# Issuing the loads of the weight sums from GpSimd's queue in the down projection of a hybrid block

## The reference, cut to what matters

```
n2 = rmsnorm(x, norm_ffn_g[l])
gate, up = jnp.split(n2 @ w_up[l], 2, axis=-1)
gate = causal_dwconv(gate, ffn_conv_w[l], ffn_conv_b[l])
x = x + (jax.nn.silu(gate) * up) @ w_down[l]
return rmsnorm(x, norm_final_g)
```

## Time and profile before

| what | us |
|---|---|
| median of 3 runs | 1129.65 |
| lowest and highest of them | 1127.28, 1418.37 |
| the profiled execution | 1126.34 |
| its span, first to last instruction | 1124.5 |
| PE, DVE, ACT, POOL busy | 1103.8, 878.1, 625.3, 53.3 |
| SP's queue of transfers, share of the 16 DMA engines | 80.1% |
| POOL's queue of transfers, the same | 0.5% |

### The profile page before, as it was taken

How to read it: one execution, slowest core, us unless ns; L and a number is a source line. 1 busy time by engine, 2 the same in 40 slices (tenths; PEclk the granted TensorE clock), 3 DMA queues, 4 the chain that set the end, 5 groups by cost and what they waited for, 6 DMA issues and landing times.

```text
span 1124.5 us, 16379 instructions
## 1 busy us (share of the span) xinstructions
PE 1103.8 (98%) x5938; PEld 946.2 (84%) x5938; DVE 878.1 (78%) x1144; ACT 625.3 (56%) x794; POOL 53.3 (5%) x46
## 2 busy tenths in 40 slices
PE   8999999999999999999999999999999999999995
PEld 8888888888888888888888888888888878777774
DVE  6778586785875677887888778788877888899796
ACT  7656475564756554344444444444444677677784
POOL 0100000000000000000000000000000000000300
PEclk9999999999999999999999999999999999999999
DMA  8877778778475578899899888988997988888984
GB/s 257 253 221 245 236 222 269 225 223 263 160 236 176 178 233 254 278 300 288 265 289 298 283 268 290 296 272 268 304 295 253 319 303 307 283 287 288 327 299 146
DMA packets 186727, 293.94 MB, mean 261 GB/s; under 512 B 9228, under 2 KB 151824, under 8 KB 182976
## 3 DMA queue, kind: packets, MB, share of 16 engines
q1 hardware_dynamic: 185664, 291.15, 80.1%
q0 software_dynamic: 448, 1.78, 0.5%
q10 hardware_dynamic: 576, 0.53, 0.1%
HBM read 261.96 MB, written 31.46 MB: 261 GB/s over the span
## 4 chain that ended last, share of the span: by engine, by line
PE 83%; DVE 9%; DMA 5%; ACT 2%; issue 1%; SPq 1%; DVEq 0%; ACTq 0%
PE ps L1465 42%; PE ps L1467 21%; PE ps L1600 12%; PE ps L1649 3%; DVE s_w L1222 2%; PE ps L1462 2%; DVE w L1222 2%; DVE w L868 2%; DMA s_raw<-w_down_dram 1%; DMA raw<-sums 1%; PE ps L1463 1%; ACT w L543 1%; DMA xres<-x_dram 1%; DMA raw<-w_down_dram 1%; DVE s_act L1222 1%; PE ps L1576 1%
## 5 line engine op out<-in xcount | busy, mean ns | idle before, releaser
L1465 PE MATMUL ps<-xT,w 128*128 128x512 f32 x2048 | 715.5, 395 | 0.6 <-DVE w L868 0.6
L543 ACT ACTIVATE w<-raw 128x1024 fp32r<-128x1024 f32 (+3 forms) x377 | 392.8, 1058 | 331.5 <-PE ps L1467 171.6
L1467 PE MATMUL ps<-xT,w 128*128 128x256 f32 x2048 | 569.1, 278 | 0.0
L868 DVE TENSOR_TENSOR w<-raw,w 128x1024 fp32r<-128x1024 f32 x332 | 407.4, 1243 | 185.9 <-ACT w L543 185.2
L1465 PEld LDWEIGHTS ps<-xT,w 128*128 128x128 f32 x2048 | 384.1, 188 | 90.0 <-issue 0.7
L1467 PEld LDWEIGHTS ps<-xT,w 128*128 128x128 f32 x2048 | 385.0, 188 | 0.3
L1600 PE MATMUL ps<-w,aT 128*128 128x512 f32 x768 | 176.9, 390 | 5.5 <-DVE aT L874 5.5
L1600 PEld LDWEIGHTS ps<-w,aT 128*128 128x128 f32 x768 | 143.2, 188 | 38.0 <-DVE w L868 7.1
L1649 PE MATMUL ps<-s_w,s_act 128*128 128x512 f32 x336 | 80.4, 394 | 2.2 <-DVE s_act L1222 2.1
L1649 PEld LDWEIGHTS ps<-s_w,s_act 128*128 128x128 f32 x336 | 62.6, 188 | 18.3 <-DVE s_act L1222 5.0
L1222 DVE TENSOR_TENSOR s_w<-s_raw,s_w 128x1024 fp32r<-128x1024 f32 (+1 forms) x48 | 65.7, 1395 | 3.6 <-ACT s_w L543 3.5
(11 more groups left out here) (177 smaller groups left out, 632.5 us busy)
## 6 DMA issues: line engine op xcount, KB each, us to landing
raw<-w_up_dram SPq DMA_DIRECT2D x176, 512.0 KB, 5.8
raw<-w_in_dram SPq DMA_DIRECT2D x92, 512.0 KB, 4.3
s_raw<-w_down_dram SPq DMA_DIRECT2D x72, 512.0 KB, 7.9
sums<-s_raw SPq DMA_DIRECT2D x56, 512.0 KB, 6.5
raw<-w_down_dram SPq DMA_DIRECT2D x44, 512.0 KB, 5.6
raw<-w_out_dram SPq DMA_DIRECT2D x32, 512.0 KB, 4.6
s_raw<-sums SPq DMA_DIRECT2D x16, 1024.0 KB, 7.5
raw<-sums SPq DMA_DIRECT2D x12, 1024.0 KB, 7.4
```

Of the source, the lines that this page charges most:

```text
L543: return sc.activation(out_, in_, fn, **kw)
L868: v.tensor_tensor(w[:, s, :, 1, :], raw[:, s, :].rearrange("p (c n) -> p c n", c=CH), w[:, s, :, 0, :], ALU.subtract).then_inc(lo_ready, 1)
L1465: mm(full, w[:, s, c, 0, cut], xT[:, kt, :, :].rearrange("p a n -> p (a n)"), start=kt == 0, stop=False)
L1467: ins = mm(rest, w[:, s, c, 1, cut], xT[:, kt, 0, :], start=False, stop=kt == KT - 1)
```

## The change

The sums of all 28 pairs are now loaded by instructions in POOL's queue (`load_sums`), with the same waits as before on DVE's steps. SP's `load_pair` issues the plain weights alone and no longer waits for the four steps. The wait on `t_stored` moves from SP to POOL. POOL's order in the down projection becomes: wait for the stored sums; sums of both runs of the first half; sums of the first run of the second half; sums of the first pair of the second run; the load of `gfin`; `xg` for r = 0; `xg` for r = 1; sums of the other six pairs. The waits of `gfin` and `xg` keep their values.

```
--- before.py
+++ after.py
@@ -304,6 +304,10 @@
 
             return 1, m, i
 
+        def sums_place(half, run, i):
+
+            return run * (2 * RUN_PAIRS) + (half * RUN_PAIRS + i)
+
         up_pairs = [(half, run, i) for half in range(2) for run in range(RUNS) for i in range(RUN_PAIRS)]
         for i in range(H):
             for m in range(MIX_SUMS if i < H - 1 else 1):
@@ -391,10 +395,6 @@
 
             down_rows = w_down.rearrange("(k p) n -> k p n", p=P)
 
-            def sums_place(half, run, i):
-
-                return run * (2 * RUN_PAIRS) + (half * RUN_PAIRS + i)
-
             def load_for_sums(half, run, i):
 
                 k = run * RUN_TILES + (RING + 2 * i)
@@ -417,7 +417,6 @@
                 dst = pair_raw[place]
                 upper = down_rows[bass.ds(k, 1), :, cols + BANK:cols + HALF].rearrange("k p n -> p (k n)")
                 lower = down_rows[bass.ds(k + 1, 1), :, cols:cols + HALF].rearrange("k p n -> p (k n)")
-                sums = sums_dram[bass.ds(sums_place(half, run, i), 1)].rearrange("t p n -> p (t n)")
                 if i == 1:
                     g = LAST_BODY[run] + (G_DOWN + half * DOWN_BODIES)
                     sp.wait_ge(lo_ready, g * RING + (RING + 2))
@@ -427,13 +426,6 @@
                     sp.wait_ge(s_lo_ready, p * S_PARTS + (1 - S_PARTS))
                 sp.dma_start(dst[:, 0:BANK], upper).then_inc(plain_landed[place], 16)
                 sp.dma_start(dst[:, BANK:BANK + HALF], lower).then_inc(plain_landed[place], 16)
-                if i == 1:
-                    sp.wait_ge(lo_ready, g * RING + 2 * RING)
-                elif i:
-                    sp.wait_ge(s_lo_ready, p * S_PARTS - S_PARTS)
-                elif half or not at_start(run):
-                    sp.wait_ge(s_lo_ready, p * S_PARTS)
-                sp.dma_start(dst[:, 2 * HALF:4 * HALF], sums).then_inc(sums_landed[place], 16)
 
             COL_Q, COL_K, COL_V, COL_O, COL_XR, COL_GR = 0, D_M, 2 * D_M, 3 * D_M, 4 * D_M + 2 * H, 4 * D_M + 2 * H + D_L
             wa_v = wa.rearrange("(i b) k j -> i k b j", b=2)
@@ -511,7 +503,6 @@
             if len(up_pairs) == UP_ITERS - 1:
                 store_sums(2 * PAIRS - 1, *up_pairs[-1])
             load_body(G_DOWN, w_down, 0, 0)
-            sp.wait_ge(t_stored, 32 * 2 * PAIRS)
 
             def load_pairs(half, run):
 
@@ -1403,16 +1394,46 @@
             with pool.Fori(0, UP_ITERS) as j:
                 after(pool, A3, "silu", j)
                 did(nc.gpsimd.tensor_tensor(fs[:], fs[:], rB[:].to_broadcast([P, 2, S]), ALU.mult), L3, "fs_r")
-            pool.wait_ge(s_used, S_STEPS * (PAIRS + RUN_PAIRS))
-            pool.dma_start(gfin, gfin_in.to_broadcast([P, D])).then_inc(gfin_landed, 16)
-            pool.wait_ge(gfin_landed, 16)
-            for r in range(ROWS):
+
+            def load_sums(half, run, i):
+
+                place, p = place_of(i), nth_pair(half, run, i)
+                if i == 1:
+                    g = LAST_BODY[run] + (G_DOWN + half * DOWN_BODIES)
+                    pool.wait_ge(lo_ready, g * RING + 2 * RING)
+                elif i:
+                    pool.wait_ge(s_lo_ready, p * S_PARTS - S_PARTS)
+                elif half or run:
+                    pool.wait_ge(s_lo_ready, p * S_PARTS)
+                pool.dma_start(pair_raw[place][:, 2 * HALF:4 * HALF], sums_dram[sums_place(half, run, i)]).then_inc(sums_landed[place], 16)
+
+            def load_gfin():
+
+                pool.wait_ge(s_used, S_STEPS * (PAIRS + RUN_PAIRS))
+                pool.dma_start(gfin, gfin_in.to_broadcast([P, D])).then_inc(gfin_landed, 16)
+
+            def weigh(r, b):
+
+                pool.wait_ge(gfin_landed, 16)
                 after(pool, A4, f"sq{r}_0")
-                pool.wait_ge(unit_used, (G_DOWN + DOWN_BODIES + r + 1) * RING + (RING + 3))
+                pool.wait_ge(unit_used, (G_DOWN + DOWN_BODIES + b) * RING + (RING + 3))
                 for n in range(2):
                     cols = slice(n * BANK, (n + 1) * BANK)
                     ins = nc.gpsimd.tensor_tensor(xg[:, r, cols], xres[:, r, cols], gfin[:, cols], ALU.mult)
                 did(ins, L4, f"xg{r}")
+
+            pool.wait_ge(t_stored, 32 * 2 * PAIRS)
+            for run in range(RUNS):
+                for i in range(RUN_PAIRS):
+                    load_sums(0, run, i)
+            for i in range(RUN_PAIRS):
+                load_sums(1, 0, i)
+            load_sums(1, 1, 0)
+            load_gfin()
+            weigh(0, 1)
+            weigh(1, 2)
+            for i in range(1, RUN_PAIRS):
+                load_sums(1, 1, i)
 
 
         @block.tensor
```

## The result

| | before | after |
|---|---|---|
| median, us | 1129.4 | 1144.44 |
| lowest, us | 1127.28 | 1141.88 |
| profiled execution and its span, us | 1126.34, 1124.5 | 1144.79, 1142.5 |

The change makes the kernel slower: 1.0135 times the time before, with an interval of 1.0111 to 1.0158. That is 15 us, against 7 us in the sum of the forecast, and just outside its range of 1125 to 1144 us.

A forecast was written before the change was run, and what follows sets the result against it. PE, busy 98% of the span, was taken as the bound, with DVE and DMA nearly full in the pairs. 1126.34 + 6.2 + 1.0 = 1133.5 us profiled, 1135 us expected as median; range 1125 to 1144 us.

The forecast's parts named there:

- Removed from SP: 28 issues of sums leave SP's queue with their waits; costed at nothing, at most some 0.3 us gain for a pair.
- The first sums: Down projection's first sums, issued after POOL's last up-projection product, land before ACT needs them: 0, at worst 0.9 us.
- The sums of a run's first pair: Issued earlier by POOL, they move beside body-weight loads at the second half's start: +1.0 us, bounds 0 to 3.5 us.
- The price of one load from POOL: Two loads of sums in the chain cost the same from POOL as from SP: 0, bounds +4.6 to -5.1 us.
- The sums behind `xg`: Last run's second-pair sums wait in POOL behind both `xg` steps, issued 10.2 us later: +6.2 us, 5.4 to 8.8.
- The clock: PE's granted clock might fall to 1.2 GHz after some 5.1 us idle in the last run: 0, 2.6 us in range.
- POOL's descriptors held by DVE: Rival: DVE delays POOL's descriptor making up to 4 us per load of sums, giving 1165 us; chance 0.09.
- Hiding: Rival: PE's stock hides the late sums of the last run's second pair, giving 1127.3 us; chance 0.06.
- gain: Rival: two queues land loads sooner and shed PE's waits in the pairs, 1126.6 or 1121 us; chance 0.15.

The follow-up runs named there:

- run 1: Not a follow-up kernel: the first of four runs of pairs in the down projection; 35.6 us in the kernel before, 37.3 us in the changed kernel.
- both parts undone: Changed kernel with `xg` for r = 1 moved behind the last six pairs' sums and early first-pair sums held back: 1.0063 times the kernel before, 7.1 us slower.
- 20 loads: Kernel before with the sums of pairs three to seven of each run loaded from POOL, `xg` for r = 1 behind them: ratio 1.0065, 7.3 us slower.
- run 4: Not a follow-up kernel: the last of four runs of pairs in the down projection; 36.2 us in the kernel before, 43.3 us in the changed kernel.
- undoing the order: Changed kernel with `xg` for r = 1 moved in POOL's order behind the loads of the last six pairs' sums: 1.0103 times the kernel before.
- The three early loads: Kernel before with first-pair sums of runs two to four issued early, from POOL (1.0036), ACT (1.0043) or SP behind the body's loads (0.9990).

## Why the prediction was wrong, by its own steps

- *Removed from SP*: nothing was forecast, and no run tests it alone.
- *The first sums*: POOL issued them at 879.38 us, 1.3 us behind the forecast by the later start of the whole; run 1 has no wait that hangs on them.
- *The sums of a run's first pair*: the step that failed first. I asked how long 1 MB takes (3.5 us) and then chose 1.0 us at one place, because the load "starts last". It doesn't: POOL issued it at 984.98 and 1047.41 us, and the body load in the chain began at 985.08 and 1047.52 us. It reached the body's last units in two places, not one, and the stages there are 4.1 and 4.0 us longer than in the first trace of before: 2.1 to 2.8 us of waiting and 1.6 us of clock at each, less the waits that stood there before. By the times it is 4 to 5 us in place of 1.0. The rows of the range held one such place; two would have been 7 us.
- *The price of one load from POOL*: the term that was mis-sized most, 0 against some 7 us (7.1 us with both parts undone, 7.3 us for 20 loads). The medians to landing of the earlier trace rows, 7.5 us for sums from SP and 7.6 us for the gain from POOL, hid it: the same comparison after the change gives

```profile
s_raw<-sums POOLq DMA_DIRECT2D x16, 1024.0 KB, 7.7
raw<-sums POOLq DMA_DIRECT2D x12, 1024.0 KB, 7.3
```

  and that looks like no cost again. "To landing" starts at the issue, and POOL's issue is itself 0.27 us later; and the price is paid in all four runs, where I had counted two loads in the chain. The upper bound of +4.6 us lies below the 5.1 to 9.1 us measured. Where most of this price comes from stays open.
- *The sums behind `xg`*: mechanism, place and order as forecast. The wait of ACT was 7.1 us (about 8 forecast) and PE's 3.6 us (about 5). The term was 6.2 us; run 4 lost 7.1 us in the trace, of which undoing the order gave back 5.8 us in the trace and 3.6 us in time.
- *The clock*: taken as 0 with 2.6 us in the range. It fell three times, for 1.6 us each at the bodies. I had looked for it behind an idle time near 5 us; here it came behind ones from 2.1 us on, at places that the sum did not have.
- *Rivals*: POOL's descriptors held by DVE by some 4 us a load did not occur; POOL's issues take 0.53 us each with DVE busy throughout, so the issue itself was not held by DVE's subtractions. That agrees with the Trainium skill's page "SBUF — State Buffer", section "Who interferes with whom", by which DVE instructions with two SBUF inputs contend with GpSimd's reads and did not hold up its descriptors. Hiding and gain did not occur either. The rule of the Trainium skill's page "DMA: Bandwidth & Descriptors", section "Issuing engines are not separate DMA queues", that only issue time is saved, fits in that nothing is won, but it was used to support a price of 0. The three early loads, 4.1 and 4.9 us from a second queue and none that shows from SP's, say that leaving the one queue is a cost where its order was the order of need.

## What to carry to other kernels

In a kernel whose loads stand in one queue in the order of need, moving some of them early to another queue can make the load that an engine needs next the late one, even if the moved one is needed by nobody yet: here three such loads cost 4.1 and 4.9 us, and none that shows in the queue of the others. Before moving a load to GpSimd, price its answer and landing at every turn of the loop that it lies in, and read GpSimd's whole program order: what stands ahead of the load there becomes its condition. If a resource is full over a stretch, it is worth a try to move large transfers out of it altogether; for the final gain here the times say 1.6 us, which their intervals do not show.

## What the runs showed of the hardware that I had not expected

- POOL starts a load 0.29 to 0.30 us after the end of the DVE instruction that it waits for; SP and ACT, where nothing else holds them, 0.02 to 0.04 us. Issuing takes 0.53 us from POOL, 0.33 us from SP and ACT, at the median.
- In the traces of the down projection the granted clock fell to 1.2 GHz after idle times of PE of 1.76, 1.82, 2.12, 2.14, 2.19 and 2.48 us, and after all seven from 2.78 to 3.61 us: its mean in the 4 us behind each was 0.57 to 0.67. It stayed at 1.00 behind idle times of 1.80, 1.81, 2.21, 2.24, 2.36 and 2.46 us. The length of the wait alone does not tell. The one of 1.76 us, from the kernel with all loads of the pairs from POOL, with 21 matmuls that take 5.09 us elsewhere:

```profile
1043.54 6.68 PE L1658 MATMUL ps<-s_w,s_act 128*128 128x512 f32 x21 [1.76 <-DVE s_act L1188]
```

- The same 20 loads of 1 MB with the same waits cost 1.1 us from ACT's queue and 7.3 us from POOL's.
